# Mixers of the second block rewritten with stationary tokens: chunks of 512 moving weight columns, rotation on GpSimd, turned queries and keys, one mask product per head

## The reference

```
dq, dk, dv, sq, sk, sv, mq, mk, mv, g_diff, g_sb, g_moba = split(h @ w_in)    # nine of width 512, three of 1024
a = rms_norm(diff_attention(rope(dq), rope(dk), dv)) * (1 - lambda_init)      # 4 heads, 2 softmax maps each
b = stick_breaking_attention(sq, sk, sv)                                      # 8 heads of 64, no rotation
c = moba_attention(rope(mq), rope(mk), mv)                                    # 8 heads of 64; causal at 256 tokens
merged = sigmoid(g_diff) * (a @ w_diff_o) + sigmoid(g_sb) * (b @ w_sb_o) + sigmoid(g_moba) * (c @ w_moba_o)
out = merged @ w_out
```

## Time and profile before

| what | value |
|---|---|
| median of three executions | 2250.84 us |
| the profiled execution's own time | 2249.25 us |
| its span, first to last instruction | 2247.4 us |
| PE busy | 2156.1 us (96%) |
| DVE, ACT, POOL busy | 1207.7, 984.1, 319.6 us |
| mean granted PE clock | 0.970 |
| split of a chunk, mean of 321: on ACT (L295), on DVE (L302) | 1913, 2352 ns |
| two mixers, from the first turn of the norm before to the start of the next network | about 328 and 331 us |

### The profile page before, as it was taken

One profiled execution on the slowest core, in us unless ns is written; L12 is line 12 of the kernel. 1 busy time (PEld: TensorE's weight loads), 2 busy tenths in 40 slices (PEclk: granted clock), 3 DMA queues, 4 the chain that ended last, 5 costly groups with the idle time before them and its releaser, 6 DMA issues.

```text
span 2247.4 us, 31714 instructions
## 1 busy us (share of the span) xinstructions
PE 2156.1 (96%) x13641; PEld 1938.2 (86%) x13641; DVE 1207.7 (54%) x1159; ACT 984.1 (44%) x1048; POOL 319.6 (14%) x186
## 2 busy tenths in 40 slices
PE   6969999999999999998999989999998999999998
PEld 6739999998999998887998978887887998897887
DVE  5545454664554554545564765545454565565553
ACT  4324343334353444434345545445444334556443
POOL 2102430223334310001110021001000130021000
PEclk9859999999999999999999999999999999999999
DMA  6105555542455546553532345554554542344553
GB/s 195 63 0 169 168 172 184 198 150 77 148 170 168 177 165 201 188 183 126 178 129 97 113 150 187 187 187 159 187 180 149 169 158 93 107 151 151 187 187 112
DMA packets 219435, 343.77 MB, mean 153 GB/s; under 512 B 5706, under 2 KB 152300, under 8 KB 219196
## 3 DMA queue, kind: packets, MB, share of 16 engines
q1 hardware_dynamic: 218684, 339.70, 45.7%
q0 software_dynamic: 368, 0.79, 0.2%
q10 hardware_dynamic: 272, 1.65, 0.2%
HBM read 341.07 MB, written 1.05 MB: 152 GB/s over the span
## 4 chain that ended last, share of the span: by engine, by line
PE 89%; DVE 4%; ACT 4%; DMA 2%; issue 1%; POOL 0%; SPq 0%; DVEq 0%; POOLq 0%
PE banks L309 15%; PE banks L311 15%; PE banks L310 15%; PE banks L460 11%; PE banks L463 11%; PE banks L461 11%; PE banks L1549 4%; PE banks L1091 2%; PE banks L1325 2%; ACT w_hi L295 1%; DVE w_lo L302 1%; PE banks L499 1%; DMA raw<-ffn_wg 1%; PE banks L1581 1%; DMA raw<-ab_w_in 1%
## 5 line engine op out<-in xcount | busy, mean ns | idle before, releaser
L302 DVE TENSOR_TENSOR w_lo<-raw,w_hi 128x2048 fp32r<-128x2048 f32 x321 | 754.4, 2352 | 529.3 <-ACT w_hi L295 529.1
L295 ACT ACTIVATE w_hi<-raw 128x2048 fp32r<-128x2048 f32 x321 | 613.5, 1913 | 758.2 <-DMA raw<-ffn_wd 154.9
L309 PE MATMUL banks<-xn_hi,w_hi 128*128 128x272 f32 (+1 forms) x2224 | 655.8, 295 | 16.1 <-DVE y L1724 6.2
L311 PE MATMUL banks<-xn_hi,w_lo 128*128 128x272 f32 (+1 forms) x2224 | 647.1, 291 | 0.0
L310 PE MATMUL banks<-xn_lo,w_hi 128*128 128x272 f32 (+1 forms) x2224 | 645.6, 290 | 0.0
L309 PEld LDWEIGHTS banks<-xn_hi,w_hi 128*128 128x128 f32 x2224 | 432.9, 195 | 21.7 <-issue 7.2
L310 PEld LDWEIGHTS banks<-xn_lo,w_hi 128*128 128x128 f32 x2224 | 433.6, 195 | 0.4
L311 PEld LDWEIGHTS banks<-xn_hi,w_lo 128*128 128x128 f32 x2224 | 432.2, 194 | 0.0
L460 PE MATMUL banks<-w_hi,xn_hi 128*128 128x512 f32 x768 | 305.5, 398 | 8.0 <-DVE w_lo L302 6.3
L461 PE MATMUL banks<-w_lo,xn_hi 128*128 128x512 f32 x768 | 302.2, 393 | 0.0
L463 PE MATMUL banks<-w_hi,xn_lo 128*128 128x512 f32 x768 | 297.0, 394 | 0.0
(11 more groups left out here) (304 smaller groups left out, 2524.0 us busy)
## 6 DMA issues: line engine op xcount, KB each, us to landing
raw<-w_in SPq DMA_DIRECT2D x60, 1024.0 KB, 5.1
raw<-ffn_w_gu SPq DMA_DIRECT2D x44, 1024.0 KB, 5.1
raw<-ffn_wd SPq DMA_DIRECT2D x44, 1024.0 KB, 4.9
raw<-ffn_wg SPq DMA_DIRECT2D x40, 1024.0 KB, 5.1
raw<-ffn_wu SPq DMA_DIRECT2D x40, 1024.0 KB, 5.1
raw<-ret_w_in SPq DMA_DIRECT2D x24, 1024.0 KB, 5.2
raw<-ffn_w_down SPq DMA_DIRECT2D x22, 1024.0 KB, 4.9
raw<-ret_w_out SPq DMA_DIRECT2D x8, 1024.0 KB, 4.9
```

Of the source, the lines that this page charges most:

```text
L295: nc.scalar.activation(w_hi[:, n0 % SLOTS, :], raw[:, n0 % SLOTS, :], ACT.Copy).then_inc(S["w_hi"], 1)
L302: nc.vector.tensor_tensor(w_lo[:, n0 % SLOTS, :], raw[:, n0 % SLOTS, :], w_hi[:, n0 % SLOTS, :].bitcast(F32), ALU.subtract).then_inc(S["w_ ...
L309: e.matmul(out, wh, xh, start=start, stop=False)
L311: return e.matmul(out, wl, xh, start=False, stop=stop)
```

## The change

Per mixer it does the following.

- **Input projection.** All 30 chunks use stationary tokens. A group is 512 columns of the projection, two chunks (`quarter(g, q, tb)`: group, half of the contraction, token block; 12 products of 512 columns). The order is the six groups of queries and keys, three of values, six of gates (`MIX_COLS`).
- **Start.** The mixer starts as the feed-forward networks do: 12 products of the first token block stand ahead of the second block's turn. The norm's factor is read as a column by token.
- **Queries and keys.** ACT takes them out of PSUM with the factor (`leave_qk`), GpSimd rotates four of the six groups in place, 16 of 64 numbers, in four instructions each, PE turns each group with eight transposes (`turn_qk`), DVE copies it (`COPY_QK`). The permutation products and the values' transposes are gone.
- **Values and gates** leave by DVE (`leave_v`, `leave_gate`).
- **Scores.** The heads are computed in pairs, first the 256-column products of both, then the 128-column ones, and one mask product of 256 columns per head covers both masked blocks.
- **Head projections and output.** Stationary tokens; gates are multiplied in token-major form, then the sum is turned by 16 transposes (`turn_merged`) that stand between the products of the output projection.
- **All four feed-forward networks of the second block and the output projection** turn the first half of the norm six products later.

```diff
@@ -561,9 +569,9 @@
             for k in (NDN - 2, NDN - 1):
                 for j2 in range(2):
                     last = down(k, j2, 1)
+                    if (k, j2) == (NDN - 1, 0):
+                        pe_turn(jp, 0, ring(f, 10))
                 last.then_inc(S["pe_chunk"], 1)
-                if k == NDN - 2:
-                    pe_turn(jp, 0, ring(f, 10))
...
         def pe_m2(l):
-            pi = 5 + 3 * l
             base = BASE[f"mix{l}"]
...
-            def narrow(n0, i, k0, halves=(0, 1)):
-                if k0 >= 2 and 0 in halves:
-                    pe.wait_ge(S["evac"], EVB[f"mix{l}"] + k0 - 1 + 4 * i)
-                pe_narrow(pe, n0, i, k0, T2, ("x2l", 16 * 3 * l + 8) if k0 == 0 else None, halves)
-                if k0 == 1:
-                    pe_stat("sa2", 3 * (3 * l + 1), T2)
...
-            def swap(gi):
-
-                for j in range(4):
-                    b = SWAP_AT[gi] + j * T2
...
+            def quarter(g, q, tb, fill=False):
+                n0 = base + 2 * g + q
+                b, slot = mix_bank(l, g) + tb, n0 % SLOTS
+                pe.wait_ge(S["w_lo"], n0 + 1)
+                for i in range(4):
+                    kt = 4 * q + i
+                    if fill:
+                        pe.wait_ge(S["x2l"], 16 * j + 8 * tb + kt + 1)
+                    w = slice(i * 512, (i + 1) * 512)
+                    last = token_product(b, tok(xn_hi, kt, tb), tok(xn_lo, kt, tb), [w_hi[:, slot, w]], [w_lo[:, slot, w]],
+                                         kt == 0, kt == KT - 1)
+                if tb:
+                    last.then_inc(S["pe_chunk"], 1)
+                elif q:
+                    last.then_inc(S["mgm"], 1)
+
+            def turn_qk(g):
+
+                if g in ROPED:
+                    pe.wait_ge(S["qrp"], 4 * l + ROPED.index(g) + 1)
+                else:
+                    pe.wait_ge(S["qev"], 12 * l + 2 * g + 2)
+                if g:
+                    pe.wait_ge(S["qcp"], 6 * l + g)
+                for n in range(4):
+                    for tb in range(2):
+                        at = 6 * 512 + n * T2 + tb * P
+                        ins = pe.transpose(ps[:, at:at + P], qn[:, g % 2, tb, n * P:(n + 1) * P], ident)
+                ins.then_inc(S["qtr"], 1)
...
             def scores(n):
                 kind, part = BATCH[n]
-
...
-                for m in (0, 1, 2, 3) if n in (0, 2, 5) else (2, 3, 0, 1):
...
+                if n == 0:
+                    pe.wait_ge(S["vev"], 3 * l + 1 + l)
+                    pe.wait_ge(S["qcp"], 6 * l + 6)
+                elif n == 4:
+                    pe.wait_ge(S["dstd"], l + 1)
+                for pair in ((0, 1), (2, 3)):
+                    if pair[0] == 2 and n:
                         pe.wait_ge(S["ov2"], 6 * l + n)
-                    q, k = qk(kind, part, m)
-                    b = (4 + m) * 512
-                    if kind == "sb":
-                        mm(ps[:, b:b + 256], k[:, 0:P], q[:, :], True)
-                        ins = mm(ps[:, b + 256:b + 384], k[:, P:T2], q[:, P:T2], False, True)
-                    else:
-                        mm(ps[:, b:b + 128], q[:, 0:P], k[:, 0:P], True)
-                        mm(ps[:, b + 128:b + 384], q[:, P:T2], k[:, :])
-                        mm(ps[:, b:b + 128], ident_r, negc_r)
-                        ins = mm(ps[:, b + 256:b + 384], ident_r, negc_r, False, True)
+                    for step in range(2):
...
+                            elif step == 0:
+                                mm(ps[:, b + 128:b + 384], q[:, P:T2], k[:, :], True)
+                            else:
+                                mm(ps[:, b:b + 128], q[:, 0:P], k[:, 0:P])
+                    if kind != "sb":
+                        for m in pair:
+                            b = (4 + m) * 512
+                            ins = mm(blocks02(ps[:, b:b + 384]), ident_r, rep(negc_r, 2, P), False, True)
                 ins.then_inc(S["sc2"], 1)
...
-                        mm(ps[:, b:b + 128], ident_r, negt_r)
-                        ins = mm(ps[:, b + 256:b + 384], ident_r, negt_r, False, True)
+                        ins = mm(blocks02(ps[:, b:b + 384]), ident_r, rep(negt_r, 2, P), False, True)
                     ins.then_inc(S["sbe"], 1)
...
+            pe_turn(j, 1, 6)
+            quarter(0, 1, 0, True)
+            quarter(1, 0, 0)
+            for q in range(2):
+                quarter(0, q, 1, True)
+            for c in range(2, 18):
+                g, q = c // 2, c % 2
+                if q == 0 and 3 <= g < 9:
+                    pe.wait_ge(S["qev"], 12 * l + 2 * (g - 3) + 2)
+                if c > 2:
+                    quarter(g, q, 0)
+                quarter(g, q, 1)
+                if c == 3:
...
+                if c in TURN_AFTER:
+                    turn_qk(TURN_AFTER[c])
...
+                if n == 0:
+                    pe.wait_ge(S["vev"], 3 * l + 2 - l)
+                elif n == 1:
+                    pe.wait_ge(S["vev"], 3 * l + 3)
+                else:
+                    pe.wait_ge(S["gev"], 6 * l + n - 1)
+                g = 9 + n
+                quarter(g, 0, 0)
+                quarter(g, 0, 1)
+                quarter(g, 1, 0)
                 turn(n)
-                narrow(base + 19 + 2 * n, 0, 19 + 2 * n, (1,))
+                quarter(g, 1, 1)
                 attend(n)
-                if n == 0:
-                    swap(3)
...
+            for x in range(2):
+                pe.wait_ge(S["m_lo"], 3 * l + x + 1)
                 for k in range(2):
-                    pe_wide(pe, BASE[f"wo{l}"] + 2 * x + k, k, 2, mo_hi[x], mo_lo[x], T2,
-                            ready=lambda j: pe.wait_ge(S["m_lo"], 3 * l + x + 1) if j == 0 and k == 0 else None,
-                            free=lambda m: bank_free(m, x))
-            pe_wout(l)
+                    for tb in range(2):
+                        if k == 0 and x == 0:
+                            pe.wait_ge(S["gev"], 6 * l + 5 + tb)
+                        elif k == 0:
+                            pe.wait_ge(S["ov2"], 6 * l + 6)
+                        project(x, k, tb, 4 + 2 * tb if x else wo_bank(l, tb))
+            pe.wait_ge(S["m_lo"], 3 * l + 3)
...
+            def turn_merged(tb, half):
+                pe.wait_ge(S["mpc"], 4 * l + 2 * tb + half + 1)
+                pe.wait_ge(S["mg"], 4 * l + 3 + tb)
+                for n in range(4):
+                    at = (4 + 2 * tb + half) * 512 + n * P
+                    c = (4 * half + n) * P
+                    ins = pe.transpose(ps[:, at:at + P], gt[:, 0, tb, c:c + P], ident)
+                ins.then_inc(S["mtr"], 1)
...
+            out(0, 0)
+            turn_merged(1, 0)
+            turn_merged(1, 1)
+            for k, tb in ((1, 0), (0, 1), (1, 1), (2, 0), (3, 0), (2, 1)):
+                out(k, tb)
+            out(3, 1, lambda: pe_turn(jw, 0, 4))
...
+            def leave_v(x):
+                for tb in range(2):
+                    half_done(6 + x, tb)
+                    b = (mix_bank(l, 6 + x) + tb) * 512
+                    ins = dve.tensor_scalar(vn2[:, tb, 512 * x:512 * (x + 1)], ps[:, b:b + 512], rcol[:, tb:tb + 1], None, ALU.mult)
+                ins.then_inc(S["vev"], 1)
...
+                if c in COPY_QK:
+                    g = COPY_QK[c]
+                    dve.wait_ge(S["qtr"], 6 * l + g + 1)
+                    dve.tensor_copy(qkT[:, 4 * g:4 * g + 4, :], ps[:, 3072:4096].rearrange("p (n t) -> p n t", t=T2)).then_inc(S["qcp"], 1)
...
+            def gated(x, tb):
+                dve.wait_ge(S["sig"], 3 * l + x + 1)
+                projected(x, tb)
+                b = (4 + 2 * tb if x else wo_bank(l, tb)) * 512
+                g = gt[:, 1 + x, tb, :]
+                dve.tensor_tensor(g, g, ps[:, b:b + 1024], ALU.mult).then_inc(S["mg"], 1)
+
+            for x in range(2):
+                for tb in range(2):
+                    gated(x, tb)
                 for k in range(2):
-                    split_lo(BASE[f"wo{l}"] + 2 * x + k + AHEAD, 0)
-                dve.wait_ge(S["sig"], 3 * l + x + 1)
...
+            def merge(tb):
+                dve.wait_ge(S["sig"], 3 * l + 3)
+                projected(2, tb)
+                if tb == 0:
+                    dve.wait_ge(S["mga"], l + 1)
+                for half in range(2):
+                    c = slice(512 * half, 512 * half + 512)
+                    b = (wo_bank(l, tb) + half) * 512
+                    g = gt[:, 0, tb, c]
+                    link(dve.tensor_tensor(g, g, ps[:, b:b + 512], ALU.mult))
+                    dve.tensor_tensor(g, g, gt[:, 1, tb, c], ALU.add).then_inc(S["mpc"], 1)
...
+            for tb in range(2):
+                merge(tb)
+                for half in range(2):
+                    merged_lo(tb, half)
...
+            def leave_qk(g):
+
+                if g >= 2:
+                    act.wait_ge(S["qtr"], 6 * l + g - 1)
...
```

(16 more changed lines are left out.)

392 lines of the change are left out of this document (187 added, 205 removed).

## The result

The changed kernel takes 2172.9 us (median of four, 2169.13 to 2174.69) against 2249.68 us for the kernel before (2248.44 to 2251.6): ratio 0.9656, 95% interval 0.9639 to 0.9673, 3.4% faster. The forecast was 2186 with a range of 2170 to 2212. In a second measurement it took 2171.85 us, ratio 0.9654 (0.9641 to 0.9667).

What follows compares the result with a forecast made beforehand. PE, busy 96%, was taken as the bound. Joins 21.5, chunks 4 to 17 11.0, batches 32.6, projections -2.6 and other turns 2.1 sum to 64.6 us off 2249.25; with 1.6 for the median, 2186, range 2170 to 2212.

Steps and rivals of the forecast that it cites:

- The rate: Mixers' products: 512 columns instead of 256 gain 0.32 us on each of 60 input chunks; chunks 4 to 17 take 82.0.
- Rival 2: Rate set by memory or records, not width: mixer chunks gain 3.7 us instead of 19.2, total 2202; chance 0.06.
- The scores: Softmax batches: a pair of heads costs 1.3 us instead of 2.44, saving 9.1 a mixer.
- Rival 1: Scores: heads do not overlap because masks or order keep pairs apart; 9.1 us per mixer lost, 2204; chance 0.11.
- What is given back: Six batches: shorter covering work exposes waits for softmax, DVE's splits and ACT's root; together 4.6 us a mixer.
- The rotation: Chunks 4 to 17: GpSimd's rotation stays hidden, a group taking 3.5 us of some 10 available.
- rival 5: GpSimd's rotation slow on strided pieces: PE stalls from 2.8 us an instruction; 2288 us at 6 each; chance 0.03.
- The projections: Head projections, output and join behind: 74.1 us against 72.85, a loss of 1.3 a mixer, including 0.8 half clock.
- Rival 4: Projections: DVE's merges wait behind splits of chunks not landed, 5.15 + 4.2 us per mixer, 2205; chance 0.11.
- The end: Kernel's end, last network: the moved turn gains 1.3 us, between 0 and 1.4.
- The clock: Half clock left in the terms: 3.4 us per mixer's batches, some in both joins, 0.8 at the projections.
- Rival 3: More half clock: batches keep their 5.1 and 9.0 us, each mixer's end loses 3 more, 2199; chance 0.16.

Runs made afterwards that it cites:

- run 1: Changed kernel with each 512-column product of the mixers' input projection issued as two of 256 columns; 2186.54 us, ratio 0.9722.
- run 2: Changed kernel with the scores' heads computed one after the other instead of in pairs, each with its one mask; 2193.17 us, ratio 0.9757.
- run 3: Changed kernel with two 128-column mask products a head instead of one of 256, still at the pair's end; 2176.16 us, ratio 0.9671.
- run 4: Kernel before with only its scores changed, to heads in pairs and one mask a head; 2222.71 us, ratio 0.9885.
- run 8: Changed kernel with three orders moved: softmax batches' weight split behind the maxima, fifth batch's heads reordered, first attention split ahead of the reciprocal; 2164.5 us, ratio 0.9631.
- run 7: Changed kernel with GpSimd's rotation made slow by 20 more multiplications a group; 2266.49 us, ratio 1.0077.
- run 5: Changed kernel with the order of the turns undone, in the second block's networks, the output projection and the mixer's start; 2181.28 us, ratio 0.9697.
- run 6: Changed kernel with the first turn six products later still, in the four networks and the output projection; 2177.78 us, ratio 0.9683.

## Why the forecast was right, and where it was too small

The time lies inside the range and faster was given 0.95; but the likeliest case's own range, 2174 to 2196, begins 1 us above it. Step by step:

- **The rate: right.** 81.81 us against 82.0, with 5.72 against 5.43 us a chunk in run 1. Rival 2 is refuted by that run.
- **The scores: right.** 1.29 a pair against 1.3; runs 2 to 4 show the overlap as its cause. The bound for the mask (3.0 a mixer) was too wide: two masks a head cost 0.15 a pair, 1.2 a mixer (run 3). The reading of 0.37 as the price of two masks took in the way back to 64 rows; with one mask a head the pair came out at 1.3 all the same. Rival 1 is refuted.
- **What is given back: right in kind and nearly in size.** The first batch's wait is 1.64 (forecast 0.4 + 1.2), the root's 1.21 (1.2), the running sums' 1.25 each (0.80 + 0.48; the list of signs said about 1.5), the third batch's 0.51 (0.8). Run 8 shows that the splits' place was the cause of the first and the third batch's waits: with it moved, each is 0.3.
- **The rotation: hidden,** as said. No turn waits for GpSimd, and run 7 shows that rival 5 would have cost about what was said.
- **The projections: a little better.** Without the 0.8 for half clock 73.3 were forecast, and 72.0 and 72.2 came. PE starts 0.82 late instead of 1.4, and the waits round the merged sum make 2.0 and 2.1 us (about 3 were forecast). The distance from the first turn to the next network's split product is 11.4 against 11.6. Rival 4 did not occur; no projection waits over 5 us for DVE.
- **The end: wrong, and small.** I gave 1.3 us for the turn moved in the last network. The last stage has the same products ahead of its second turn in either order, and nothing behind them; the distance from the start of that network to its last turn changed by 1.2, all of it in its first 18 us, by the clock. The gain was 0, the lower bound. Behind the last turn the end even grew from 7.9 to 8.3 us: the last sixteen transposes, at half clock, took 3.5 us instead of 2.3.
- **The clock: the step that failed.** Three times the sum left half clock in place: "I estimate 3.4 us of loss left per mixer" in the batches, the 18.48 us "half clock included" in both joins, and "0.8 for one more half-clock stretch". In the profile there was none left in either mixer. In the batches that is 6.8 us, more than the 5.7 by which they beat the forecast; in the joins 17.21 stands for 18.48 (2.5 us of the 2.9); at the projections 1.6 of the 4.3; and the networks behind gained 1.2 each in the same way. Together (5.7 + 2.5 + 1.6 + 2.4) some 12 of the 15.5 us between forecast and profile; 1.2 more lie ahead of the change, where nothing was changed. Rival 3 had the clock as the uncertain thing and looked only to the other side, with 0.16 for more half clock and nothing for none at all, though the text names "none lost" as the own range's lower end.

The batches' term was wrong in both profiles of the changed kernel, and all other versions with pairs agree but for two pieces (run 4). The joins' terms were wrong only in some profiles. A join with a piece takes 29.8 us, which is nearly the 30.1 that the sum gave it, and seven of the 18 unchanged joins have one (run 5). That both joins of the changed kernel's profiles were free of it is in part luck: both profiles are the fastest executions of their runs, and the median lies 3.8 us above the first, the price of about two pieces.

Why the clock rose is shown for one part, the long scores of single heads: removed from the kernel before, the half clock of the batches went (run 4), put back, it returned (run 2). For the idle time round the turns at the joins it is only likely (run 5). By the clock columns of the earlier trace rows the kernel before spent the equivalent of 27.9 us on half clock in the six windows under 1.00 shown there, idle time included, and the changed kernel's profile none; so between these two profiles some 13 (run 4) to 28 of the 80 us are the clock. What stays open is why one wait brings half clock and another of the same length does not: the wait of 2.1 us at the joins is in every version, and the clock falls behind it in some profiles and joins and not in others with the same instructions.

## What to carry to other kernels

In this kernel two heads' products, on opposite halves of the array's rows, ran at once only where nothing that uses all rows stood between them: order heads in pairs, and put their masks at the pair's end. Where a clock column is under 1.00 in a stretch, price its return as a term with both signs: an edit that shortens low work can give back the clock too, here between a sixth and a third of the gain. Before a piece of half clock is put down to an edit, look whether stretches that the edit leaves alone show such pieces in other profiles. And when the covering work gets shorter, look again at what stands in order ahead of the critical step on each helper engine; three such moves gave 6 to 8 us more (run 8).

## What the runs showed that I had not expected

- A wait costs more than its length: four waits of 38.5 us together made the products of the stretch 8.5 us longer (run 7).
- Going from full-height products back to 64-row ones has a price: from mask to 64-row product 0.31 us pass with one 256-column mask, 0.44 with two, and only 0.22 from one mask to a full-height product (run 2). With two 128-column masks it is 0.37, with four 0.59 (run 3), so a mask of 128 columns costs 0.11, hardly less than the 0.13 of one of 256.
- The output's join takes 11.4 us from the first turn whether 30 or 24 products of PE lie in it (run 6).
